# Two-pass layer entries, a third home for converted weights, and an attention whose value products follow the first scores

## The reference, cut to what matters

```python
hx = modulate(rms_norm(x, norm_mix_pre[l]), sh1x, sc1x)      # hc likewise for the context
z  = hx @ w_in[l]            # one projection for three head groups
y  = concat(gated_delta_net(z), latent_attention(z), hgrn2(z)) @ w_out[l]
x  = x + g1x * rms_norm(y, norm_mix_post[l])
x  = x + g2x * rms_norm(relu(modulate(rms_norm(x, ...)) @ w_mlp1[l]) ** 2 @ w_mlp2[l], norm_mlp_post[l])
```

## Time and profile before

| | |
|---|---|
| median of 3 runs | 2359.84 us (2358.8 to 2365.69) |
| profiled execution, its time | 2362.27 us |
| profiled execution, its span | 2360.3 us |
| TensorE busy | 2254.1 us, 95% |
| VectorE, ScalarE, GpSimd busy | 50%, 37%, 9% |
| mean granted TensorE clock | 0.987 |

### The profile page before, as it was taken

The page is one execution under the profiler, slowest core; times in us unless marked ns, Lnnn a source line. Parts: engine busy times, 40 slices in busy tenths (PEclk is TensorE's granted clock), DMA queues, the critical chain, the costliest instruction groups (busy, mean ns, idle before and its releaser), DMA issues.

```text
span 2360.3 us, 43150 instructions
## 1 busy us (share of the span) xinstructions
PE 2254.1 (95%) x19324; PEld 1825.2 (77%) x19324; DVE 1176.4 (50%) x1848; ACT 862.7 (37%) x1250; POOL 219.3 (9%) x204
## 2 busy tenths in 40 slices
PE   8999999989999999999999999889998999999998
PEld 5876598876668788888888677558785669888887
DVE  4674353288363651424233577536248456444444
ACT  5362134125453421212123545232324455322233
POOL 3013410000120100000000021421000211000000
PEclk9999999999999999999999999999998999999999
DMA  8218101134301121212121221410216302323222
GB/s 317 63 55 267 44 25 62 54 109 140 103 17 37 36 89 55 72 54 72 54 72 55 100 64 42 149 53 19 72 55 211 119 7 66 107 89 105 92 90 71
DMA packets 161694, 198.42 MB, mean 84 GB/s; under 512 B 18358, under 2 KB 129432, under 8 KB 160871
## 3 DMA queue, kind: packets, MB, share of 16 engines
q1 hardware_dynamic: 155536, 185.20, 24.3%
q10 hardware_dynamic: 5271, 10.10, 1.3%
q0 software_dynamic: 704, 0.37, 0.2%
HBM read 184.60 MB, written 11.06 MB: 83 GB/s over the span
## 4 chain that ended last, share of the span: by engine, by line
PE 86%; DVE 7%; ACT 4%; issue 2%; POOL 0%; DMA 0%; DVEq 0%; ACTq 0%
PE ps L1534 35%; PE ps L849 16%; PE ps L1452 5%; PE ps L1068 3%; PE ps L1396 2%; PE ps L883 2%; PE ps L942 2%; PE ps L1491 2%; PE ps L1207 1%; PE ps L836 1%; DVE region L2490 1%; PE ps L827 1%; PE ps L1409 1%; PE ps L1426 1%; PE ps L1092 1%
## 5 line engine op out<-in xcount | busy, mean ns | idle before, releaser
L1534 PE MATMUL ps<-region_r 128*128 128x512 f32 (+1 forms) x1536 | 377.0, 354 | 0.0
L1534 PEld LDWEIGHTS ps<-region_r 128*128 128x128 f32 x1536 | 270.7, 188 | 40.5
L1534 PE MATMUL ps<-region_r,weights_r 128*128 128x512 f32 (+1 forms) x768 | 229.9, 354 | 0.0
L2141 DVE TENSOR_TENSOR weights_r<-weights,region_r 128x2048 fp32r<-128x2048 f32 x62 | 141.9, 2289 | 120.2 <-ACT region_r L1670 120.2
L1534 PE MATMUL ps<-mixed_r,weights_r 128*128 128x512 f32 (+1 forms) x672 | 201.2, 354 | 0.0
L1534 PE MATMUL ps<-modulated_r,region_r 128*128 128x256 f32 (+1 forms) x624 | 186.8, 354 | 0.0
L1534 PE MATMUL ps<-mixed_r,region_r 128*128 128x256 f32 (+1 forms) x624 | 186.7, 354 | 0.0
L1534 PEld LDWEIGHTS ps<-region_r,weights_r 128*128 128x128 f32 x768 | 144.6, 188 | 20.3
L2070 ACT ACTIVATE region<-ps,cst 128x768 f32<-128x768 f32 (+1 forms) x64 | 50.3, 796 | 297.7 <-PE ps L1534 279.7
L2645 DVE TENSOR_TENSOR region_r<-region 128x768 fp32r<-128x768 f32 (+1 forms) x64 | 52.8, 824 | 201.1 <-ACT region L2070 201.1
L1534 PEld LDWEIGHTS ps<-mixed_r,weights_r 128*128 128x128 f32 x672 | 126.5, 188 | 17.9
(11 more groups left out here) (421 smaller groups left out, 4754.0 us busy)
## 6 DMA issues: line engine op xcount, KB each, us to landing
weights<-in_w_mlp SPq DMA_DIRECT2D x64, 1024.0 KB, 5.6
weights<-in_w_ada SPq DMA_DIRECT2D x40, 1024.0 KB, 5.3
weights<-in_w_in SPq DMA_DIRECT2D x34, 1024.0 KB, 5.3
region<-in_w_ada SPq DMA_DIRECT2D x8, 1024.0 KB, 17.3
weights<-in_w_out SPq DMA_DIRECT2D x8, 1024.0 KB, 6.6
x_kept<-residual SPq DMA_DIRECT2D x2, 3072.0 KB, 12.4
region<-decays_kept ACTq DMA_DIRECT2D x4, 1536.0 KB, 11.3
residual<-x_kept SPq DMA_DIRECT2D x2, 3072.0 KB, 10.1
```

The source lines that it names most:

```text
L1534: last = mm(dst[:, CTX + a:CTX + b], w[:, k, m], r[:, a:b], start=(k == 0 and r is r_low), stop=(k == KB - 1 and w is low))
L2141: v.tensor_tensor(ring_r[:, at, :], ring[:, at, :], mlp_high(j), ALU.subtract).then_inc(w_low_ready, 1)
```

## The change

- **Two passes.** The new `gemm_entry` takes the first load (layer 0) or the first two loads (layer 1). It runs, for all blocks, the products with high tokens, waiting for `q_high_ready`, and then, for all blocks, those with low tokens, waiting for `q_low_ready`. Before it stand 4 (layer 0) or 6 (layer 1) clock holds. In layer 1 VectorE does all eight multiplications before the eight differences.
- **A third home.** The high part of load 2 goes to `R_r[:, 5, 0:2048]` and waits for no earlier products. In layer 1 its conversion moves ahead of the entry on ScalarE, and right behind the differences on VectorE.
- **Attention.** Two scores come right behind the query units, each waiting for its own head's rotation, then the six value products, into the unused columns of banks 6, 7 and 4. ScalarE takes two values, runs the first exponential, takes two more, the second exponential and the last two. VectorE rotates three heads, and the fourth after the first normalization. The conversion `out_high_part(l, 0)` moves behind the fourth exponential. Holds are 1, 1, 1, 1 (layer 0) and 1, 1, 1, 0, with none before the first score.
- **GpSimd.** Its work beside the attention starts after the eighth exponential in layer 0 and after the fourth in layer 1, and the 2048-column difference is written as eight of 256 columns, in both layers.

```diff
@@ proj_high
-                z = R_r[:, 3, 0:2048] if s % 2 else S_r[...]
+                z = R_r[:, 5, 0:2048] if s == 2 else R_r[:, 3, 0:2048] if s % 2 else S_r[...]
@@ GpSimd
+                pool.wait_ge(pe_ready, ATT0[l] + (2 * H if lo == 0 else 4))
...
-                        nc.gpsimd.tensor_tensor(ring_r[:, at, :], ring[:, at, :], out_w_high[0], ALU.subtract).then_inc(y_parts_early, 1)
+                        for n in range(8):
+                            piece_of = slice(256 * n, 256 * n + 256)
+                            last = nc.gpsimd.tensor_tensor(ring_r[:, at, piece_of], ring[:, at, piece_of], out_w_high[0][:, piece_of], ALU.subtract)
+                        last.then_inc(y_parts_early, 1)
@@ TensorE, entry
+            def gemm_entry(l, loads, lo):
+
+                units = [u for i in loads for u in (2 * i, 2 * i + 1)]
+                dst = [free_pair(l, "qkv", u) for u in units]
+                hold_clock(dst[0][:, 512:1024], 4 + 2 * l)
+                weights = [list(parts(l, "qkv", i)) for i in loads]
+                for k in range(KB):
+                    pe.wait_ge(q_high_ready, 8 * l + k + 1)
+                    for j, u in enumerate(units):
+                        m = slice(128 * (u % 2), 128 * (u % 2) + 128)
+                        for n, w in enumerate(weights[j // 2]):
+                            for a, b in streams(lo):
+                                mm(dst[j][:, CTX + a:CTX + b], w[:, k, m], q_high[k][:, a:b], start=(k == 0 and n == 0), stop=False)
+                for k in range(KB):
+                    pe.wait_ge(q_low_ready, 8 * l + k + 1)
+                    for j, u in enumerate(units):
+                        m = slice(128 * (u % 2), 128 * (u % 2) + 128)
+                        for a, b in streams(lo):
+                            last = mm(dst[j][:, CTX + a:CTX + b], weights[j // 2][0][:, k, m], q_low[k][:, a:b], start=False, stop=(k == KB - 1))
+                        if k == KB - 1:
+                            last.then_inc(gemm_out, 1)
...
-                for i in range(3):
-                    gemm_parts(l, "qkv", i, [2 * i, 2 * i + 1], q_high, q_low, lo if i < 2 else 0, q_low_ready if i == 0 else None)
+                entered = (1, 2)[l]
+                gemm_entry(l, range(entered), lo)
+                for i in range(entered, 3):
+                    gemm_parts(l, "qkv", i, [2 * i, 2 * i + 1], q_high, q_low, lo if i < 2 else 0)
@@ TensorE, attention
-                for ci in range(NC):
-                    dst = free_pair(l, "vt", ci)
-                    mm(dst[:, 512:768]..., CKV[:, 128 * ci:128 * ci + 128], wv[:, :, 64:128], ...).then_inc(gemm_out, 1)
-                hold_clock(pair(number(UNITS, l, "out", 0))[:, 512:1024], 1 + l)
-                pe.wait_ge(gemm_evac, number(UNITS, l, "vt", NC - 1) + 1)
-                pe.wait_ge(rope_done, 5 * (l + 1))
...
-                FIRST_HOLDS = ((2, 2, 1, 1), (2, 1, 1, 0))
-                scores(0)
-                scores(1)
+                FIRST_HOLDS = ((1, 1, 1, 1), (1, 1, 1, 0))
+                pe.wait_ge(kr_copied, l + 1)
+                for i in range(2):
+                    pe.wait_ge(gemm_evac, number(UNITS, l, "uq", 1 + i) + 1)
+                    scores(i)                    # waits rope_done >= 5 * l + 2 + i for i < H
+                for ci in range(NC):
+                    pe.wait_ge(gemm_evac, number(UNITS, l, "uq", 0 if ci < 4 else 3) + 1)
+                    mm(value_rows(ci)..., CKV[:, 128 * ci:128 * ci + 128], wv[:, :, 64:128], ...).then_inc(gemm_out, 1)
...
+                    if i == 0:
+                        pe.wait_ge(gemm_evac, number(UNITS, l, "vt", NC - 1) + 1)
@@ ScalarE, attention
-                for ci in range(NC):
-                    copied(l, "vt", ci, af(VT[:, ci, :], finished(l, "vt", ci)[:, 512:768], ACT.Copy))
-                act.wait_ge(rope_done, 5 * (l + 1))
-                out_high_part(l, 0)
...
+                for ci in range(2):
+                    take_values(ci)
                 probabilities(0)
+                for ci in range(2, 4):
+                    take_values(ci)
                 for i in range(len(steps)):
                     if i + 1 < len(steps):
                         probabilities(i + 1)
+                    if i == 0:
+                        for ci in range(4, NC):
+                            take_values(ci)
+                    if i == 2:
+                        act.wait_ge(rope_done, 5 * (l + 1))
+                        out_high_part(l, 0)
@@ ScalarE, between the layers
                     proj_high_part(l + 1, 1)
+                    proj_high_part(l + 1, 2)
@@ VectorE, entry of layer 1
-                    for b in range(KB + 2):
-                        if b < KB:
-                            v.tensor_tensor(Hm[:, b, :], X[:, b, :], rs, ALU.mult).then_inc(xn_ready, 1)
-                        if b >= 2:
-                            q_low_block(l, b - 2)
+                    for b in range(KB):
+                        v.tensor_tensor(Hm[:, b, :], X[:, b, :], rs, ALU.mult).then_inc(xn_ready, 1)
+                    for b in range(KB):
+                        q_low_block(l, b)
+                    proj_low_part(l, 2)
@@ VectorE, attention
-                for h in range(H):
+                for h in range(H - 1):
+                    rotate_queries(h)
...
+                    if i == 0:
+                        rotate_queries(H - 1)
```

More of the change, by code:

```diff
@@ L507, in trunk_program, with value_rows @@
         PT = [R[:, 4, 2 * TOK:3 * TOK], R[:, 4, 3 * TOK:4 * TOK], R[:, 0, 2 * TOK:3 * TOK], R[:, 0, 3 * TOK:4 * TOK]]
+        def value_rows(ci):
+            return ps[:, (6, 6, 7, 7, 4, 4)[ci], 256 * (ci % 2):256 * (ci % 2) + 256]
         HQ, HV, HGT = blocks(0), R[:, 1, 0:NC * 256].rearrange("p (c e) -> p c e", c=NC), R[:, 1, 2 * TOK:4 * TOK].rearrange("p (b t) -> p b t", b=2)
@@ L851, in products @@
                 return last
+            def gemm_entry(l, loads, lo):
[18 more added lines that the diff above has]
+                            last.then_inc(gemm_out, 1)
             def gemm_parts(l, what, load, units, r_high, r_low, lo=0, r_ready=None):
                 dst = [free_pair(l, what, u) for u in units]
-                if what == "qkv" and load == 0:
-                    hold_clock(dst[0][:, 512:1024], 5 + l)
                 high, low = parts(l, what, load)
@@ L1376, in _ @@
                     last.then_inc(gemm_out, 1)
-                wv = arrived(l, "ukv")[:, 0:512].rearrange("p (h n) -> p h n", h=H)
-                for ci in range(NC):
-                    dst = free_pair(l, "vt", ci)
-                    mm(dst[:, 512:768].rearrange("p (h n) -> p h n", h=H), CKV[:, 128 * ci:128 * ci + 128], wv[:, :, 64:128],
-                       start=True, stop=True).then_inc(gemm_out, 1)
-                pe.wait_ge(gemm_evac, number(UNITS, l, "out", 0) - 3)
-                hold_clock(pair(number(UNITS, l, "out", 0))[:, 512:1024], 1 + l)
-                pe.wait_ge(gemm_evac, number(UNITS, l, "vt", NC - 1) + 1)
-                pe.wait_ge(rope_done, 5 * (l + 1))
-                pe.wait_ge(kr_copied, l + 1)
                 steps = att_steps(l)
@@ L1391, in scores @@
                     a = ATT0[l] + i
+                    if i < H:
+                        pe.wait_ge(rope_done, 5 * l + 2 + i)
                     if i >= 2:
@@ L1411, in output @@
                     last.then_inc(pv_out, 1)
-                FIRST_HOLDS = ((2, 2, 1, 1), (2, 1, 1, 0))
-                scores(0)
-                scores(1)
+                FIRST_HOLDS = ((1, 1, 1, 1), (1, 1, 1, 0))
[3 more added lines that the diff above has]
+                    scores(i)
+                wv = arrived(l, "ukv")[:, 0:512].rearrange("p (h n) -> p h n", h=H)
+                for ci in range(NC):
+                    pe.wait_ge(gemm_evac, number(UNITS, l, "uq", 0 if ci < 4 else 3) + 1)
+                    mm(value_rows(ci).rearrange("p (h n) -> p h n", h=H), CKV[:, 128 * ci:128 * ci + 128], wv[:, :, 64:128],
+                       start=True, stop=True).then_inc(gemm_out, 1)
                 for i, (qt, h) in enumerate(steps):
@@ L1653, in proj_high_part @@
                 act.wait_ge(w_in_s[n % NSLOT], landed(n))
-                if 2 <= s < 7 or 9 <= s < 15:
+                if 3 <= s < 7 or 9 <= s < 15:
                     act.wait_ge(*weights_used(LOADS.index((l, *PROJ[s - 2]))))
@@ L1775, in _ @@
                     padded(u)
-                    if u % 2 == 1:
+                    if u % 2 == 1 and (l == 0 or u > 1):
                         proj_high_part(l, (2, 3, 4, 6)[u // 2])
@@ L2270, in _ @@
                 for u in range(8):
-                    if u in (1, 3, 5, 6, 7):
+                    if u in (1, 3, 5, 6, 7) and (l == 0 or u > 1):
                         proj_low_part(l, {1: 2, 3: 3, 5: 4, 6: 5, 7: 6}[u])
```

6 lines of the change are left out of this document (5 added, 1 removed).

## The result

The changed kernel took 2344.68 us (median of 6 runs, 2339.98 to 2346.88) against 2360.60 for the one before (6 runs, 2356.65 to 2365.69): ratio 0.9935, 95% interval 0.9922 to 0.9948, so 15.9 us faster. Measured again beside other kernels it took 2348.26 (6 runs), 0.9957 (0.9945 to 0.9970) of the kernel before, 11.0 faster.

A forecast was written before the change was run, and what follows sets the result against it. TensorE, busy for 95% of the span, was taken to bound the kernel. Gains 1.6 + 5.2 - 0.2 + 2.3 + 2.1 = 11.0 below 2359.84 gave 2348.8 us; own range 2345.5 to 2352, all cases 2343.5 to 2355.5.

The forecast's parts named there:

- Layer 0 entry: First projection of layer 0: high-token products run first, waiting for copies only; gain 1.6 us, bounds 0.3 to 1.8.
- Layer 1 entry: First projection of layer 1: two loads share both passes, ending at 1382.2 against 1387.4; gain 5.2 us, bounds 3.5 to 5.8.
- the falling clock: Sign of being wrong: the granted clock falls at 1340 us or in an attention.
- The third home: Load 2's conversion before layer 1's squares delays the first by 1.9 us; cost 0.2 (0 to 0.8), nothing in layer 0.
- The cold-clock rival: Half-clock stretches after layer 1's holds or in attention cost up to 1.7 us each, two or three 4: 2353; chance 0.13.
- Layer 0 attention: Attention of layer 0: earlier start 4.4 us less port losses 2.1; net gain 2.3, bounds 0.4 to 4.4.
- the port loss: Layer 0's attention: normalizations wait for GpSimd at the shared port in four exposed steps; 2.1 us taken, 0 to 4.
- the 4.4: Layer 0's attention: the first 768-wide transpose comes at 662.3 instead of 666.67, 4.4 us earlier.
- GpSimd takes the attention gain back: Rival, both attentions: every exposed normalization waits a whole 1.8 or 1.3 us; gain sum 5.1, 2354.7; chance 0.10.
- Layer 1 attention: Attention of layer 1: first transpose 3.3 us earlier, less 1.2 for GpSimd's work beside six steps; net gain 2.1.
- The slower rival: GpSimd wins the port in all 14 attention steps, losing 21.3 us instead of 3.3, end 2366.8; chance 0.03.
- starts counting fully: Rival, entries and attentions: no port losses, copies at their best, gains sum to 15.3 us, 2344.5; chance 0.12.

The follow-up runs named there:

- the kernel with three edits: Changed kernel with load 2's conversion behind the modulations and entry holds asking for three bank pairs (layer 1), GpSimd waiting in layer 0 alone; 2344.86 us (0.9948).

## Why the prediction was right, and where by luck

**Layer 0 entry, 1.6.** Right: 1.62 to the next load, with the first product at 46.41 (46.8 forecast) and the end 16.8 us later. Another 0.6 that I didn't foresee lies behind it: ScalarE takes the units of loads 1 and 2 every 8.32 us instead of 8.48 (load 1) and 8.37 (load 2). It comes with the entries (-2.19) and not with the attention (0.00). What shortens these products is open.

**Layer 1 entry, 5.2.** Mis-sized: 2.95. The core of the sum was right, a load pair dense at 0.23 per product and load 2 starting 23.3 us after the first product (23.1 forecast). Two steps ahead of it were left out. The holds come behind the root's evacuation, since four units take all pairs: 0.76, by the run that undid it. And the idle stretch that I had put among the rivals did come, with the falling clock that I had named as a sign of being wrong: 1.54 of half clock. 2.95 + 1.54 + 0.76 = 5.25, which the kernel with three edits reached.

**The third home, 0.2.** Right as to ScalarE and TensorE being level again at the last square (0.0 where the clock stayed up); wrong where the clock falls. The cold-clock rival was true in place and size (1.54 against "up to 1.7"), but for one stretch.

**Layer 0 attention, 4.4 - 2.1 = 2.3.** The net was mis-sized: 4.49 measured. The term that failed is the port loss, "2.1 taken, 0 to 4": it was some 0.5 (5.0 gained at the first 768-wide transpose, 4.5 at the last); the start gave 0.6 more than the 4.4. Nor is the 2.1 the sum of its own terms: one step at 0.36 and three at 0.75 make 2.6, and in layer 1 two at 0.36 and two at 0.5 make 1.7, not 1.2. I treated meetings of normalization and GpSimd as random with an average wait, though both queues are periodic: in the changed kernel every second copy begins 5.84 to 5.86 us after the one before (660.33, 666.17, 672.03), every second normalization 5.85 to 5.86 (666.79, 672.65, 678.50), so their phase stays. Both hold each other: in the phase of the changed kernel, too, every second copy lasts 1.15 instead of 0.82, and every second difference 2.01. The changed kernel fell into a good phase, by luck. Started earlier, later by one step or by two, or with one long piece, the same work costs 1.5 to 6.2 more (one step later not by its phase but by one long meeting and the half clock behind it). The rival "GpSimd takes the attention gain back" describes what the others did; where GpSimd started decided it, and not an average. Also, the 4.4 are not the order's own: alone it loses 0.9, since it needs GpSimd out of the early steps.

**Layer 1 attention, 2.1.** Right in sum (2.15). Its parts differ: the order gives 2.33 with GpSimd as before, the pieces 0.5 more, the wait takes 0.7 back.

**The sum.** 2.2 + 4.5 + 2.95 + 2.15 = 11.8, less 1.6 when the clock falls in layer 0's MLP, plus 0.6 where the units of layer 0's output projection are the shorter ones: 10.2 to 12.4, against 11.0 forecast. That the sum came out is luck in part, for two errors cancelled: 2.2 too little in layer 0's attention, 2.2 too much in layer 1's entry. The first measurement gave 15.9, the second 11.0; over all runs the medians are 2345.88 (12) and 2359.89 (42, one of 6975 us left out), 14.0. So 1.6 to 3.8 us lie beyond the stages, and what they are is open. In the recurrences the other thirteen traces, my experiments' with them, stand 3.0 below the one of before on average (1.87 and 1.17); but that execution was itself 2.4 above its median, so most of the 3.0 may be its own. Whether the change also makes the clock fall less often there can't be settled with one trace of the kernel before.

**The chances.** The slower rival never came near. That of starts counting fully (2344.5, chance 0.12) has the first measurement's time, but not its sum: layer 1's entry gave 2.95 of the 5.8, and the rest came from outside the stages.

## What to carry to other kernels

When two engines share a port and both run in cycles, don't price their meetings by the average: work out the phase, and try the start earlier and later, since the same work differed by 1.5 to 6.2 us here. Order and cover must be tried together: in layer 0 the order alone lost 0.9 us, the cover alone gained 1.0, and both gained 4.5. And when work is moved ahead of a chain, look for the idle stretch it opens on TensorE: the delay itself was made good, the low clock behind it was not.

## What the runs showed of the hardware

- The clock falls behind waits of TensorE, not always. After idles of 3.08, 2.94, 2.77 and 1.81 us the granted clock was 0.50 to 0.53 in a stretch that began between 0.3 us before and 1.2 us after their end; after the same 2.94 us it stayed up in three of ten traces, and after an idle of 1.86 in layer 0's MLP in seven of 14. Behind the idle of 1.14 us in the kernel with the late conversion the squares ran at full clock too.
- Such a stretch turns one program into two lengths: 12.28 or 10.74 us for 32 products; 0.0 or 1.6 us in layer 0's MLP (half clock at 798.8 in the changed kernel, none in the run with one load in two passes).
- A normalization of 0.62 us lasts 1.8 for several steps in a row when it begins 0.4 us after each of GpSimd's differences of 1.81, and 0.6 to 1.2 in the other phase. Each side delays the other (GpSimd's copy 1.16 instead of 0.82), which keeps them in step.
- A `tensor_reduce` of VectorE that reads PSUM took its usual 0.94 us in the middle of a GpSimd difference of 4.54.
- Eight GpSimd differences of 256 columns took 5.65 to 6.57 us together, the one of 2048 columns 4.54.
- The same ScalarE instruction, compared between executions of different kernels, repeats to 0.05 us per stage where clock and program are the same and the pair of 8.32 and 8.48 above stands at the same value, though whole times of one kernel scatter by up to 15.
